# First projection of a conformer block: three column groups multiplied by depth, two steps behind each modulation pair

## The reference, cut to what is touched

```python
c_act = jax.nn.silu(c)
mod = c_act @ mod_w[i] + mod_b[i]
sh_m, sc_m, gt_m, sh_f, sc_f, gt_f = [m[:, None, :] for m in jnp.split(mod, 6, axis=-1)]
h = rmsnorm(x, norm_pre_mix[i]) * (1.0 + sc_m) + sh_m
...
def conformer_conv_module(h, w1, b1, dw_w, dw_b, ln_g, ln_b, w2, b2):
    u = h @ w1 + b1                      # 1024 -> 2048
    a, gt = jnp.split(u, 2, axis=-1)
    u = a * jax.nn.sigmoid(gt)
    u = causal_dwconv(u, dw_w) + dw_b    # 31 taps
    u = jax.nn.silu(layernorm(u, ln_g, ln_b))
    return u @ w2 + b2
```

## Time and profile before

| | |
|---|---|
| median of 3 runs | 1487.47 us (1482.71 to 1488.34) |
| span of the profiled execution | 1487.0 us |
| what lies around that span, against the median | 0.5 us |
| PE busy | 1432.8 us, 96% of the span |
| DVE, ACT, POOL busy | 64%, 46%, 11% |

### The profile page before, as it was taken

The page is one execution under the profiler, slowest core; times in us unless marked ns, Lnnn a source line. Parts: engine busy times, 40 slices in busy tenths (PEclk is TensorE's granted clock), DMA queues, the critical chain, the costliest instruction groups (busy, mean ns, idle before and its releaser), DMA issues.

```text
span 1487.0 us, 31275 instructions
## 1 busy us (share of the span) xinstructions
PE 1432.8 (96%) x12734; PEld 1301.1 (88%) x12734; DVE 950.1 (64%) x1266; ACT 684.0 (46%) x864; POOL 161.7 (11%) x180
## 2 busy tenths in 40 slices
PE   5999979999999999999999999999999999999997
PEld 4877679999999998998888999989999899899996
DVE  2655566666755557596778565675656678855656
ACT  3444554545533445754435333454343566533432
POOL 1342032322000003003300000000000012000000
PEclk8999989999999999999999999999999999999999
DMA  9975446666666664431016666666666444576662
GB/s 364 324 256 200 140 128 200 181 188 183 180 185 190 183 189 124 151 133 32 32 59 184 195 183 187 188 173 191 185 196 184 132 153 142 151 217 189 184 187 90
DMA packets 297972, 257.73 MB, mean 173 GB/s; under 512 B 7072, under 2 KB 274336, under 8 KB 294816
## 3 DMA queue, kind: packets, MB, share of 16 engines
q1 hardware_dynamic: 297888, 256.49, 56.8%
HBM read 255.42 MB, written 1.05 MB: 172 GB/s over the span
## 4 chain that ended last, share of the span: by engine, by line
PE 48%; DVE 5%; ACT 1%; issue 1%; DVEq 0%; ACTq 0%
PE ps L140 14%; PE ps L141 14%; PE ps L142 14%; PE ps L2068 3%; ACT arena L444 1%; DVE stats L330 1%; DVE arena L328 1%; DVE arena L401 0%; PE ps L2051 0%; PE ps L378 0%; PE ps L2059 0%; DVE gate_m L2371 0%; PE ps L2553 0%; DVE a_parts L2775 0%; PE ps L2541 0%
## 5 line engine op out<-in xcount | busy, mean ns | idle before, releaser
L140 PE MATMUL ps<-actT,a_parts 128*128 128x256 f32 x2176 | 615.0, 283 | 10.2 <-DVE actT L406 4.5
L141 PE MATMUL ps<-actT,a_parts 128*128 128x256 f32 x2176 | 610.5, 281 | 0.0
L142 PE MATMUL ps<-actT,a_parts 128*128 128x256 f32 x2176 | 609.9, 280 | 0.0
L140 PEld LDWEIGHTS ps<-actT,a_parts 128*128 128x128 f32 x2176 | 412.2, 189 | 21.7 <-issue 10.3
L141 PEld LDWEIGHTS ps<-actT,a_parts 128*128 128x128 f32 x2176 | 412.2, 189 | 4.2
L142 PEld LDWEIGHTS ps<-actT,a_parts 128*128 128x128 f32 x2176 | 412.0, 189 | 0.0
L1139 DVE TENSOR_TENSOR a_parts<-a_raw,a_parts 128x2048 fp32r<-128x2048 f32 x100 | 239.1, 2391 | 55.7 <-ACT a_parts L1136 55.3
L1153 DVE TENSOR_TENSOR b_parts<-b_raw,b_parts 128x1024 fp32r<-128x1024 f32 x72 | 88.2, 1225 | 160.5 <-ACT b_parts L1150 160.5
L1136 ACT ACTIVATE a_parts<-a_raw 128x2048 fp32r<-128x2048 f32 x100 | 190.3, 1903 | 0.0
L1150 ACT ACTIVATE b_parts<-b_raw 128x1024 fp32r<-128x1024 f32 x90 | 95.3, 1059 | 171.1 <-PE ps L142 171.1
L142 PE MATMUL ps<-b_parts,hid 128*128 128x512 f32 x400 | 158.3, 396 | 0.0
(11 more groups left out here) (360 smaller groups left out, 1712.8 us busy)
## 6 DMA issues: line engine op xcount, KB each, us to landing
a_raw<-in_ffn_w_gate SPq DMA_DIRECT2D x88, 512.0 KB, 4.0
a_raw<-in_ffn_w_up SPq DMA_DIRECT2D x88, 512.0 KB, 5.2
b_raw<-in_ffn_w_down SPq DMA_DIRECT2D x88, 512.0 KB, 3.3
arena<-in_mod_w SPq DMA_DIRECT2D x24, 1024.0 KB, 8.2
a_raw<-in_f_up_w SPq DMA_DIRECT2D x44, 512.0 KB, 5.1
b_raw<-in_f_down_w SPq DMA_DIRECT2D x22, 512.0 KB, 3.4
a_raw<-in_rwkv_w_in SPq DMA_DIRECT2D x10, 1024.0 KB, 5.4
a_raw<-in_sb_w_in SPq DMA_DIRECT2D x10, 1024.0 KB, 5.1
```

Of the source, the lines that this page charges most:

```text
L140: pe.matmul(out, lhs[0], rhs[0], start=start, stop=False)
L141: pe.matmul(out, lhs[0], rhs[1], start=False, stop=False)
L142: return pe.matmul(out, lhs[1], rhs[0], start=False, stop=stop)
```

## The change

The weights of the first projection are loaded in another cut. The first three column groups (`DEEP`) come by depth: four chunks of 0.75 MB, each with two of the eight depth blocks of all three groups. The groups 3 to 6 keep their form (`pw1_cols`), and group 7 comes as two chunks of half the size. `split_hi` and `split_lo` work on the width of a chunk only (1536, 2048 or 1024 columns). Depth step `u - 1` is multiplied during unit `u` (36 matmuls in pieces of 18, 9 and 9, between the two sums, behind the second and behind `mod_post`) into the three banks 4, 5 and 6. These are among the banks in which the turned `x` stands, so it is copied out first, by DVE and ACT, and each bank is opened by a matmul of one row by a tile of zeros. Step 3 and group 3 follow, and the loop behind them takes its units from 4 on, with the groups 4 to 7 after the passes 0, 1, 3 and 5.

```diff
-    up("pw1", A["a_pw1_w"][0], [[(j * P, j * P + P), (D + j * P, D + j * P + P)] for j in range(KD)])
+    for u in range(KD // 2):
+        ring_a.append([((n * 2 * WIDE, (n + 1) * 2 * WIDE), ("p (k n) -> p k n", {"k": 2}),
+                        v[:, 2 * u:2 * u + 2, n * D:n * D + WIDE]) for n in range(2)])
+    up("pw1_cols", A["a_pw1_w"][0], [[(j * P, j * P + P), (D + j * P, D + j * P + P)] for j in range(DEEP, KD - 1)] +
+       [[(n * D + (KD - 1) * P, n * D + KD * P)] for n in range(2)])
...
-                    for i in range(4):
-                        load_mod(sp, i)
-                    ring_a.load(sp, g_pw1)
-                    for i in range(4, 8):
-                        load_mod(sp, i)
-                    ring_a.load(sp, g_pw1 + 1)
+                    for u in range(4):
+                        for i in unit_chunks(u):
+                            load_mod(sp, i)
+                        ring_a.load(sp, g_pw1 + u)
+                    ring_a.load(sp, g_cols)
                     sp.dma_start(par[:, n_first:], A["par"][:, n_first:]).then_inc(rest_loaded, 16)
...
                     act.wait_ge(xn_turned, 2)
+                    act.activation(hT[:, 4:6], turned[:, 4:6], ACT.Copy).then_inc(high_copied, 1)
+                    act.activation(hT[:, 6:8], turned[:, 6:8], ACT.Copy).then_inc(high_copied, 1)
+                    act.wait_ge(low_copied, 2)
                     for u in range(4):
                         for i in unit_chunks(u):
                             mod_take(act, i)
+                        act.wait_ge(post_read, u + 1)
                         if u == 2:
-                            ring_a.split_hi(act, g_pw1)
-                        act.wait_ge(post_read, u + 1)
+                            act.wait_ge(high_copied, 2)
                         for k in range(2 * u, 2 * u + 2):
-                            ins = act.activation(hT[:, k], turned[:, k], ACT.Identity, bias=mod_cols[:, 0, k:k + 1],
+                            ins = act.activation(hT[:, k], hT[:, k], ACT.Identity, bias=mod_cols[:, 0, k:k + 1],
                                                  scale=mod_cols[:, 1, k:k + 1])
                         ins.then_inc(affine_done, 1)
+                        ring_a.split_hi(act, g_pw1 + u)
+                    ring_a.split_hi(act, g_cols)
...
+                    def deep(u, groups):
+                        for k, j, n in groups:
+                            at = n * 2 * WIDE + (k % 2) * WIDE + j * P
+                            w = [ring_a.part(g_pw1 + u, s, at, at + P) for s in range(2)]
+                            ins = mm3(pe, ps[:, 4 + j, n * SEQ:(n + 1) * SEQ], w,
+                                      [actT[:, s, k] for s in range(2)], False, n == 1 and k == KD - 1)
+                        return ins
+                    def deep_wait(u):
+                        ring_a.wait_split(pe, g_pw1 + u)
+                        pe.wait_ge(input_done, u + 1)
...
                     for u in range(4):
-                        for i in unit_chunks(u):
-                            mod_sum(pe, i)
-                        if u < 3:
-                            mod_post(pe, u)
-                    ring_a.wait_split(pe, g_pw1)
-                    project(0, 0, [0, 1])
-                    mod_post(pe, 3)
-                    project(0, 0, range(2, KD))
-                    project(0, 1, range(KD)).then_inc(ring_a.used, 1)
-                    for j in range(1, KD):
+                        before = by_depth(u - 1) if u else []
+                        mod_sum(pe, 2 * u)
+                        if u:
+                            deep_wait(u - 1)
+                            deep(u - 1, before[0:6])
+                        mod_sum(pe, 2 * u + 1)
+                        if u:
+                            deep(u - 1, before[6:9])
+                        mod_post(pe, u)
+                        if u == 0:
+                            pe.wait_ge(low_copied, 2)
+                            pe.wait_ge(high_copied, 2)
+                            for j in range(DEEP):
+                                pe.matmul(ps[:, 4 + j], ident[0:1], zeros[0:1, 0:512], start=True, stop=False)
+                        else:
+                            deep(u - 1, before[9:]).then_inc(ring_a.used, 1)
+                    deep_wait(3)
+                    for j in range(DEEP):
+                        ins = deep(3, [(k, j, n) for n in range(2) for k in (KD - 2, KD - 1)])
+                        ins.then_inc(proj_done if j < DEEP - 1 else ring_a.used, 1)
+                    project(DEEP)
...
                     for u in range(4):
                         mod_columns(dve, u)
-                        if u == 2:
-                            ring_a.split_lo(dve, g_pw1)
                         dve.wait_ge(affine_done, u + 1)
...
+                        ring_a.split_lo(dve, g_pw1 + u)
```

More of the change, by code:

```diff
@@ L106, in __init__ @@
             self.load_no.append(loads[g % 2])
+        self.width = [max(span[1] for span, _, _ in dmas) for dmas in chunks]
     def load(self, sp, g):
@@ L553, in mod_sum @@
                 if i >= 2:
-                    pe.wait_ge(mod_taken, i - 1)
+                    pe.wait_ge(mod_taken, i if 17 <= i < 20 else i - 1)
+                if 8 <= i < 16 and i % 2:
+                    pe.wait_ge(post_read, i // 2)
                 for k in range(KD):
@@ L733, in shifts, with sigmoid @@
                         ins.then_inc(shift_act, 1)
-                    act.wait_ge(rest_loaded, 16)
-                    for j in range(KD):
-                        ring_a.split_hi(act, g_pw1 + j + 1)
+                    def sigmoid(j):
+                        if j < DEEP - 1:
+                            act.wait_ge(proj_done, j + 1)
+                        else:
+                            ring_a.wait_used(act, last_chunk(j))
+                        act.activation(sig[:, j % 2], ps[:, 4 + j % DEEP, SEQ:2 * SEQ], ACT.Sigmoid,
+                                       bias=col("a_pw1_b", KD + j)).then_inc(sig_done, 1)
+                    act.wait_ge(rest_loaded, 16)
+                    sigmoid(0)
+                    sigmoid(1)
+                    shifts(0)
+                    shifts(1)
+                    ring_a.split_hi(act, g_cols + 1)
+                    SPLIT_AT = {0: [g_cols + 2], 1: [g_cols + 3], 2: [g_cols + 4], 4: [g_cols + 5],
+                                6: [g_mem], 7: [g_mem + 1]}
+                    for j in range(KD):
+                        for i in unit_chunks(UNIT_AT[j]):
+                            mod_take(act, i)
+                        for g in SPLIT_AT.get(j, ()):
+                            ring_a.split_hi(act, g)
+                        conv_out(j)
                         if j == 4:
@@ L740, in _ @@
                             act.activation(mem_parts[:, 0], mem_raw, ACT.Copy).then_inc(mem_hi, 1)
[L741 to L752, removed]
+                        if j + 2 < KD:
+                            sigmoid(j + 2)
+                            shifts(j + 2)
                     for k in range(KD):
@@ L840, in _ @@
                     for u in range(4):
[L841 to L857 removed]
+                        before = by_depth(u - 1) if u else []
[12 more added lines that the diff above has]
+                                pe.matmul(ps[:, 4 + j], ident[0:1], zeros[0:1, 0:512], start=True, stop=False)
+                        else:
+                            deep(u - 1, before[9:]).then_inc(ring_a.used, 1)
[4 more added lines that the diff above has]
+                    project(DEEP)
+                    PROJECT_AFTER = {0: 4, 1: 5, 3: 6, 5: 7}
+                    for j in range(KD):
+                        for i in unit_chunks(UNIT_AT[j]):
                             mod_sum(pe, i)
@@ L860, in _ @@
                             mean(j - 2)
-                        convolve(j - 1)
-                        mod_post(pe, unit)
-                    mod_sum(pe, unit_chunks(11)[0])
+                        convolve(j)
+                        mod_post(pe, UNIT_AT[j])
+                        if j in PROJECT_AFTER:
+                            project(PROJECT_AFTER[j])
                     mean(KD - 2)
-                    convolve(KD - 1)
-                    mod_post(pe, 11)
                     ring_a.wait_split(pe, g_mem)
```

86 lines of the change are left out of this document (56 added, 30 removed).

## The result

The changed kernel takes 1496.32 us (median of 8 runs, 1490.99 to 1498.45), the kernel before 1487.9 us in the same comparison (1482.71 to 1490.99). The ratio is 1.0051, with a 95% interval of 1.0036 to 1.0065. The forecast was 1497 us, in a range of 1488 to 1504. The time of an execution is 1.7 us above its span (the profiled one has 1498.02 and 1496.3), not 0.5 as I read from the median before, so the two profiles are best compared by their spans: 1496.3 against 1487.0, 9.3 us more.

A forecast was written before the change was run, and what follows sets the result against it. The prediction took PE, busy for 96% of 1487.0 us, as the bound. It added 2.1 us for the chain and 8.1 for the clock, 1497.2, and with the runs' median 0.5 above the span said 1497 us, range 1488 to 1504.

The forecast's parts named there:

- The common point: State with four units and 144 projection matmuls done: 58.5 us against 56.4 before, without falls; PE full behind it.
- later loads: Loads issued up to 15 us later could starve the convolution loop; case shared with lasting low clock, 1502 to 1510, chance 0.10.
- The signs that the prediction names: Trace of steps 0 to 3: waits of 2 to 3 us, starts at least 10 us apart, changing clock, end near 66.
- The start of step 0: First depth step of the projection, after its weights are split: could start at 24.2 us.
- the three one-row matmuls: Bank opening on PE before step 0: 3.9 us, taken from four such matmuls in the trace at 5.26 us.
- The cycle: From one depth step to the next: 10.0 us at the high clock, PE working 7.1 and waiting 2.9, three times.
- the late parameters: Remaining parameters queued on SP behind a load waiting until near 44 us: in by 54, cost taken at nothing.
- The clock: PE falling to the low clock around the depth steps: three falls of 2.7 us, 8.1 us in all.
- the chain: Depth steps each hanging on the one before through sums, affine step and weight splits: 2.1 us later than before.
- four falls: By the skill's rule, clock falls behind the one-row matmuls and in all three waits: 10.8 us in place of 8.1.
- The transfers: Loads for the depth steps: not the limit; first ones there near 22 us, last chunk before 34, needed near 44.
- The overlap: Faster rival, chance 0.11: splits done while PE works, 144 matmuls done near 50.6 us, time 1477 to 1482 us.

The follow-up runs named there:

- cheap_open: Changed kernel with the three bank-opening one-row matmuls read as bf16: 1496.41 us, ratio 1.0046 to the kernel before.
- filled_waits: Changed kernel with identity matmuls on PE ahead of the waits for steps 1, 2 and 3: 1494.64 us, ratio 1.0043 to the kernel before.
- pool_late: Changed kernel with POOL's first tap table begun only after the low part of step 3's weights: 1496.61 us, ratio 1.0072 to the kernel before.
- all_filled: Changed kernel with bf16 bank opening, POOL's first table late and identity matmuls in all four waits: 1491.38 us, ratio 1.0029 to the kernel before.
- split_first: Changed kernel with weights split ahead of the affine step on ACT and DVE in units 0 to 3: 1487.87 us, ratio 1.0007 to the kernel before.
- sums_cheap_again: Five-round repeat of the changed kernel with sums and `mod_post` ahead of the depth step on PE and bf16 bank opening: 1479.72 us, ratio 0.9952.

## Why the prediction was right, point by point

**The common point.** It held. Span less mark is 1425.0 us in the kernel before (1487.0 - 62.0) and in the changed one (1496.3 - 71.3), and 1423.8 to 1426.1 in nine of the ten others. In cheap_open it is 1421.9 (1495.0 - 73.1). Behind the mark the clock falls twice more in every profile, near 146 to 168 us and near 181 to 204, and stays low for a time that differs: after the first of these for 3.4 us in cheap_open, for 6.8 in the kernel before. So a comparison by the mark is good to some 2 us. The loop of convolutions hid all else; later loads did no harm. The signs that the prediction names came as well: the last of the 36 matmuls of step 3 ends near 71.3 - 5.6 = 65.7 us (near 66 forecast), the clock changed twice between 20 and 60 us, and the three waits end with the low part of the weights, two of them in the range of 2 to 3 us.

**The start of step 0.** Forecast 24.2, measured 25.53. The weights' low part was there at 23.6 (forecast 24.1), so it was PE that came late: the three one-row matmuls took 4.9 us, not 3.9, and the sum behind them 1.9, not 1.0, for the clock fell at 19.4. This term was 1.3 us too small in this profile. In filled_waits and pool_late, where the clock fell only behind them (at 21.0 and 20.7), the same three matmuls took 2.84 us and step 0 began at 22.80 and 22.54 us. The 3.9 us were scaled from a row at mixed clock, and fit neither case.

**The cycle.** Forecast 10.0 at the high clock with a wait of 2.9; measured 10.23 (37.59 to 47.82) with 2.65. Each of its terms is in the trace: 1.47 for the high part, 1.76 for the low.

**The step that was missing.** Step 3 came 11.49 us after step 2, not 10.2: POOL's tap table, started by the late parameters, lay on DVE's subtraction. The prediction took the late parameters at nothing. Pool_late shows 1.3 us.

**The clock.** Forecast three falls of 2.7 us, 8.1 in all. The profile has two, not three. The first lies on step 0 and on the first cycle (12.06 us against 10.23), with the 1.3 us above 3.1 us; the second on step 3, 20 matmuls at 0.213 for 0.117, 1.9 us. Together 5 us. With 2.1 for the chain, 0.6 for three cycles that are 0.2 longer, and POOL's 1.3 that is 9.0 of the 9.3 us. That the sum of 10.2 us met the 9.3 us measured is partly luck: the clock was 3 us too high, the cycle (0.6) and POOL (1.3) too low. Over the executions the clock's part is smaller still. All_filled is under the changed kernel by 4.9 us in the medians (1496.3 against 1491.4) and by 3.3 us in the ratios (1.0051 against 1.0029); less POOL's 1.3 that leaves 2.0 to 3.6 us, in which the cheaper opening is contained. What stays without any low clock before the mark is the 4.0 us of all_filled over the kernel before, where the forecast had 2.1 for the chain. The mechanism was right, its division into chain and clock was not. Small slips in the prediction's arithmetic (6.9 MB should be 6.8, a cycle of 14.3 us 14.2, and 1497.2 + 0.5 is 1497.7) change nothing.

**Why it falls.** The prediction counted the one-row matmuls as a place of their own for a fall. Cheap_open doesn't bear that out: without them the clock falls just as well, in the wait that takes their place. What decides a fall is open: some came in waits, some within the one-row matmuls, in which PE shows as busy (19.00 to 20.00 us: 1.00, at clock 0.70). By the rule of the Trainium skill, page TensorE: Matmul & The Clock Gate, section HAM oscillation — how this bites in real kernels, each group starts cold where a group of matmuls is shorter than the wait for its operands. The prediction drew four falls from it. But by its own numbers PE works 7.1 us in a cycle and waits 2.9, so the condition isn't met and the rule as quoted gives none. The runs lie between: two waits of 2.65 us in cheap_open (falls at 34.4 and 48.0 us) and two in pool_late (34.3, which is 0.9 us behind the end of its wait, and 44.6) cost the clock, two of 2.64 and 2.65 us in the changed kernel's own profile did not.

**The rivals.** The transfers were not the limit: between 18 and 71 us no wait of PE in the changed kernel names a chunk, and DMA stood at 0.47 and 0.22. The overlap that the prediction put at 1477 to 1482 us exists, but not by the place of the splits: split_first only comes level with the kernel before. It takes the order on PE together with the cheap opening, at 1481.6 and 1479.7 us; the order alone gives 1485.07, whose interval ends at 1.0000.

## What to carry to other kernels

Before work is put into another stage's waits, look at what is queued behind it on the same engine. Here the sums that feed the next unit stood behind matmuls that waited for weights, so hidden work turned into a chain that was longer than the transfers it should hide under. Put the instructions that others wait for ahead of the filling work, and count a handoff over three engines as a cycle, not as a latency. Where PE rests a few microseconds per cycle, count the clock too, as a spread and not as a number.

## What the runs showed of the hardware

- Waits of 2.65 us cost the clock in two profiles (two each in cheap_open and pool_late), and two waits of 2.64 and 2.65 us did not in a third (the changed kernel). Runs of cheap_open spread over 10.8 us, of sums_cheap_again over 2.8 us.
- Matmuls of the identity in the waits kept the clock at 1.00 from 20 to 60 us (all_filled); that kernel, which also has the bf16 opening and POOL late, is 4.9 us under the changed one in the medians (3.3 us in the ratios), though its fill computes nothing.
- A POOL multiplication of 128x1024 made a DVE subtraction of 128x512 take 2.28 us in place of 0.69, where the two overlapped (the changed kernel, with pool_late as the control).
